# A two-part network on one core: another order of splits, squares and head factors in the hybrid projections, and closing products whose first weight unit goes chunk by chunk

## The reference

```python
h = rmsnorm_2(x, g_mix)
proj = h @ w_in
fq, fk, fv = ...              # 512 columns each: 8 heads of 64
q = rmsnorm_2(q, q_gain)      # per head
k = rmsnorm_2(k, k_gain)
log_f = jax.nn.log_sigmoid(f_logit + b_f)
cum_f = jnp.cumsum(log_f, axis=1)
s = q @ k.T * scale + cum_f[query] - cum_f[key]     # causal
outs.append(softmax(s) @ v)
```

## Time and profile before

| | |
|---|---|
| median of three runs | 2404.61 us (2401.77 to 2405.07) |
| profiled execution, its own time | 2405.37 us |
| its span in the profile | 2403.4 us |
| TensorE busy | 2305.6 us, 96% of the span |
| VectorE, ScalarE, GpSimd busy | 1136.2, 871.9, 363.4 us |

### The profile page before, as it was taken

One profiled execution on the slowest core, in us unless ns is written; L12 is line 12 of the kernel. 1 busy time (PEld: TensorE's weight loads), 2 busy tenths in 40 slices (PEclk: granted clock), 3 DMA queues, 4 the chain that ended last, 5 costly groups with the idle time before them and its releaser, 6 DMA issues.

```text
span 2403.4 us, 26105 instructions
## 1 busy us (share of the span) xinstructions
PE 2305.6 (96%) x10864; PEld 1871.0 (78%) x10864; DVE 1136.2 (47%) x1746; ACT 871.9 (36%) x1290; POOL 363.4 (15%) x319
## 2 busy tenths in 40 slices
PE   7789999999979999999998999999999999999998
PEld 5457888888857678888887867888888788888886
DVE  4894433334224645334345465554233346555552
ACT  4664322223213643222143275552322234333342
POOL 1301210112200002011031302332001111000021
PEclk8799999999989999999999999999999999999999
DMA  3203232323251012232335123225244333332331
GB/s 125 93 13 106 90 103 90 104 88 110 71 175 61 1 50 91 88 105 88 105 79 88 18 23 65 52 46 88 53 88 92 101 89 87 106 105 88 97 97 61
DMA packets 218882, 197.04 MB, mean 82 GB/s; under 512 B 5216, under 2 KB 211500, under 8 KB 218637
## 3 DMA queue, kind: packets, MB, share of 16 engines
q1 hardware_dynamic: 216748, 189.70, 29.8%
q0 software_dynamic: 1504, 5.51, 0.7%
q10 hardware_dynamic: 513, 0.17, 0.0%
HBM read 190.65 MB, written 4.72 MB: 81 GB/s over the span
## 4 chain that ended last, share of the span: by engine, by line
PE 87%; DVE 6%; ACT 4%; DMA 2%; issue 1%; POOL 0%; SPq 0%; POOLq 0%; ACTq 0%; DVEq 0%
PE bank L519 23%; PE bank L521 23%; PE bank L520 23%; PE bank L2091 5%; PE bank L842 2%; PE bank L2277 2%; PE bank L1596 1%; PE bank L693 1%; DVE dsa_latents L1155 1%; DVE small L1153 1%; DVE weight_lo L505 1%; PE bank L1021 1%; PE bank L703 1%; PE bank L1438 1%; ACT hybrid_step L806 1%
## 5 line engine op out<-in xcount | busy, mean ns | idle before, releaser
L519 PE MATMUL bank<-h_hi,weight_hi 128*128 128x512 f32 (+1 forms) x1576 | 622.1, 395 | 12.0 <-DVE weight_lo L505 5.2
L520 PE MATMUL bank<-h_lo,weight_hi 128*128 128x512 f32 (+1 forms) x1576 | 617.3, 392 | 0.0
L521 PE MATMUL bank<-h_hi,weight_lo 128*128 128x512 f32 (+1 forms) x1576 | 617.2, 392 | 0.0
L505 DVE TENSOR_TENSOR weight_lo<-weight_raw,weight_hi 128x2048 fp32r<-128x2048 f32 (+2 forms) x183 | 387.3, 2116 | 410.9 <-ACT weight_hi L496 410.8
L496 ACT ACTIVATE weight_hi<-weight_raw 128x2048 fp32r<-128x2048 f32 (+2 forms) x183 | 321.4, 1756 | 393.6 <-PE bank L521 350.6
L519 PEld LDWEIGHTS bank<-h_hi,weight_hi 128*128 128x128 f32 (+1 forms) x1576 | 298.2, 189 | 76.7 <-issue 11.3
L521 PEld LDWEIGHTS bank<-h_hi,weight_lo 128*128 128x128 f32 (+1 forms) x1576 | 297.9, 189 | 63.8
L520 PEld LDWEIGHTS bank<-h_lo,weight_hi 128*128 128x128 f32 (+1 forms) x1576 | 298.3, 189 | 62.2 <-issue 0.2
L519 PE MATMUL bank<-hidden_hi,weight_hi 128*128 128x512 f32 x512 | 201.8, 394 | 0.0
L521 PE MATMUL bank<-hidden_hi,weight_lo 128*128 128x512 f32 x512 | 200.7, 392 | 0.0
L520 PE MATMUL bank<-hidden_lo,weight_hi 128*128 128x512 f32 x512 | 198.7, 388 | 0.0
(11 more groups left out here) (407 smaller groups left out, 3158.9 us busy)
## 6 DMA issues: line engine op xcount, KB each, us to landing
weight_raw<-in_w_down SPq DMA_DIRECT2D x40, 1024.0 KB, 5.1
weight_raw<-in_w_up SPq DMA_DIRECT2D x32, 1024.0 KB, 5.4
weight_raw<-in_w_up SPq DMA_DIRECT2D x44, 512.0 KB, 4.6
weight_raw<-in_w_in SPq DMA_DIRECT2D x20, 1024.0 KB, 9.0
weight_raw<-in_w_in SPq DMA_DIRECT2D x26, 512.0 KB, 7.1
weight_raw<-in_w_kv_shared SPq DMA_DIRECT2D x6, 1024.0 KB, 4.9
weight_raw<-in_w_branch SPq DMA_DIRECT2D x6, 1024.0 KB, 5.0
weight_raw<-in_a_w_o SPq DMA_DIRECT2D x4, 1024.0 KB, 6.4
```

The costliest lines, as they stand in the source:

```text
L505: dve.e.tensor_tensor(split_flat(v, 1), raw_flat(v), f32(split_flat(v, 0)), ALU.subtract).then_inc(*split.mark(("unit", v)))
L519: pe.e.matmul(o, w[0], x[0], start=start, stop=False)
L520: pe.e.matmul(o, w[0], x[1], start=False, stop=False)
L521: return pe.e.matmul(o, w[1], x[0], start=False, stop=stop)
```

## The change

Two things are changed. In `product_to_stream` the first unit is written chunk by chunk as well: both tiles' banks are opened at once, and chunk k is multiplied into both before chunk k+1. In `mix` and at the start of `fox` the same instructions stand in another order on TensorE, ScalarE and VectorE.

```diff
         def product_to_stream(pe, name, source, freed, ready, st):
-            n = tile = 0
+            n, tile = 1, unit_by_chunk(pe, name, 0, 0, source, freed, ready)
...
+            sums = {2: [0], 3: [1], 4: [2, 3], 6: [4], 7: [5]}
+            spreads = {5: [0], 6: [1, 2], 7: [3]}
             for t in range(2, 8):
                 product_tile(pe, ("fox", t), ...)
-                if t < 6:
-                    tensor_head_sums(pe, t - 2)
-                if t > 4:
-                    tensor_head_spread(pe, t - 5)
-                if t == 7:
-                    tensor_head_sums(pe, 4)
-            tensor_head_spread(pe, 3)
+                for n in sums.get(t, []):
+                    tensor_head_sums(pe, n)
+                for n in spreads.get(t, []):
+                    tensor_head_spread(pe, n)
             for t in range(NT):
                 tensor_fox_values(pe, 0, t)
-                if t < 3:
-                    tensor_head_sums(pe, 5 + t)
+                if t == 0:
+                    tensor_head_sums(pe, 6)
+                    tensor_head_sums(pe, 7)
...
             square(0)
             square(1)
-            scalar_log1p_exp(act, mix, "forget", fl, fe, fu, (mix.dve, ("forget_rows",)))
-            for t in range(2, 8):
-                round_upto(act, unit_at["fox", t // 2] + 1)
-                square(t)
-                if t == 5:
-                    root(0)
-            for t in range(NT):
+            round_upto(act, unit_at["fox", 2])
+            scalar_log1p_exp(act, mix, "forget", fl, fe, fu, (mix.dve, ("forget_rows",)), lambda: square(2))
+            square(3)
+            round_upto(act, unit_at["fox", 3])
+            root(0)
+            square(4)
+            square(5)
+            round_upto(act, unit_at["fox", 4])
+            square(6)
+            square(7)
+            take_values(0, 0)
+            root(1)
+            take_values(0, 1)
+            round_upto(act, unit_at["fox", 5])
+            for t in range(2, NT):
                 take_values(0, t)
-            root(1)
-            round_upto(act, unit_at["fox", 5])
...
+            split_upto(dve, unit_at["fox", 2])
             take(2)
-            vector_log1p_exp(dve, mix, "forget", fe, fu, fd, fox_zero)
-            split_upto(dve, unit_at["fox", 2])
-            take(3)
+            vector_log1p_exp(dve, mix, "forget", fe, fu, fd, fox_zero, lambda: take(3))
+            split_upto(dve, unit_at["fox", 3])
...
+            head_factors(0)
+            take(4)
...
-            take(4)
-            split_upto(dve, unit_at["fox", 3])
             take(5)
-            head_factors(0)
             head_norm(0)
+            split_upto(dve, unit_at["fox", 4])
             take(6)
-            split_upto(dve, unit_at["fox", 4])
...
+            head_factors(1)
             split_upto(dve, unit_at["fox", 5])
-            head_factors(1)
...
         def fox_tensor(pe):
+            for t in range(2):
+                tensor_fox_values(pe, 1, t)
             for h in range(FOX_HEADS + 2):
...
-                if h < 2:
-                    for t in (2 * h, 2 * h + 1):
+                if h == 0:
+                    for t in range(2, NT):
                         tensor_fox_values(pe, 1, t)
```

More of the change, by code:

```diff
@@ L1707, in build_program, with scalar_log1p_exp @@
         ab = const[:, C_FOXAB:C_FOXAB + 4]
-        def scalar_log1p_exp(act, st, name, x, e, u, after):
+        def scalar_log1p_exp(act, st, name, x, e, u, after, between=None):
             by, what = after
@@ L1715, in scalar_log1p_exp, with vector_log1p_exp @@
             act.e.activation(e, e, ACT.Exp, scale=-1.0).then_inc(*st.act.mark((name, "exp")))
+            if between:
+                between()
             act.wait_ge(*st.dve.when(name, "below"))
             act.e.activation(u, u, ACT.Ln).then_inc(*st.act.mark((name, "log")))
-        def vector_log1p_exp(dve, st, name, e, u, d, z):
+        def vector_log1p_exp(dve, st, name, e, u, d, z, between=None):
             dve.wait_ge(*st.act.when(name, "exp"))
```

## The result

The changed kernel runs in 2377.94 us (median of 4 runs, 2377.44 to 2380.47), the kernel before in 2403.49 us (4 runs, 2401.77 to 2405.07): ratio 0.9896, 95% interval 0.9883 to 0.9909. I had said 2382 with a range of 2379 to 2389.

What follows compares the result with a forecast made beforehand. TensorE, busy for 96% of the span, was taken as the bound, so only its idle and slow time could be won. 22.2 + 0.8 + 0.7 = 23.7 us off the profiled 2405.4 gave 2381.7, said as 2382, range 2379 to 2389.

Steps and rivals of the forecast that it cites:

- The three stalls: TensorE idles in `mix` before tile 4 (5.20 us), the first spread (3.5) and the last four spreads (5.89); all go.
- all the signs named for a right forecast: No L693, tile 4 split or second L2677 wait; `mix` clock 1.00; tile 4 to spreads 45 us; values 23 us earlier.
- The links between them: In `mix`, splits, roots and copies would be ready before TensorE wants them: slack 5 us for `fox 2`, 7 for `fox 3`.
- 22.2 for `mix`: Tile 4 to the last spreads ends 22.2 us earlier: 14.6 of idle time, 7.6 of slow stretches behind it.
- 0.8 for the head loop: Value tiles before head 1's logits bring the first product with the values forward by 0.8 us more.
- The 3.05 in this term: Start of the head loop: head 1's logits 1.8 us, the last maximum 0.69, and 0.5 between them.
- 0.7 for o_2: In the closing product o_2, three matmuls of tile 1 fill the second wait, at chunk 1: 0.7 us.
- nothing for the attentions: The two attentions' closing products show no such TensorE wait, so the edit there was costed at nothing.
- No link was late: Rival: a late link, the first spread in `mix` the tightest, costs 5.8 us if all comes back: 2387.5; chance 0.15.
- The meetings of VectorE and GpSimd: Rival: at the head loop's start the two block each other; three meetings cost 2.1 us: 2384; chance 0.08.
- The chunkwise unit's matmuls: Rival: alternating banks delays the first units' 144 matmuls; from 0.16 us each the gain is gone; chance 0.02.

Runs made afterwards that it cites:

- before_again: The kernel before with no edit, run as if it were a changed one: 2402.96 us, ratio 0.9999.
- close_again: The kernel before with only the new chunk-by-chunk closing products (`product_to_stream`), the same edit as close_only: 2402.24 us, ratio 0.9994.
- again: The changed kernel with no edit, run once more against the kernel before: 2377.41 us, ratio 0.9891.
- late_roots: The changed kernel with the first root put back behind tile 5's square and the first head factors behind the take of tile 5: 2384.92 us.
- late_split: The changed kernel with `fox 2` rounded and split behind the forget chain again: 2387.54 us.
- old_head: The changed kernel with the old start of the head loop, the value tiles of the second half behind the first logits again: 2381.81 us, ratio 0.9911.
- close_only: The kernel before with the new `product_to_stream` alone: 2401.06 us, ratio 0.9989.

## Why the prediction was right about the place and wrong about the range

**The three stalls.** Right. Each has been shown by putting it back, and all the signs named for a right forecast came. The links between them held: the split of `fox 2` ends at 1288.31 + 2.29 = 1290.6 and that of `fox 3` at 1300.38 + 2.28 = 1302.7 in the trace of after; the prediction, moved by the 0.9 us by which `mix` starts earlier in this trace, had 1291.5 - 0.9 and 1303.6 - 0.9:

```profile
1288.31 2.29 DVE L505 TENSOR_TENSOR weight_lo<-weight_raw,weight_hi 128x2048 fp32r<-128x2048 f32 x1
...
1300.38 2.28 DVE L505 TENSOR_TENSOR weight_lo<-weight_raw,weight_hi 128x2048 fp32r<-128x2048 f32 x1
```

**22.2 for `mix` and 0.8 for the head loop.** Together 23.0 against 22.7 measured. (The old order took 108.74 to 109.57 us in six traces, the new one 86.70 in four, so 22.5 on average.) By the end of the spreads 67.5 - 45.85 = 21.7 us were won, 0.5 less than the sum: I had put every small group at the 0.80 us of a head sum, but the eight spreads took 6.97 us and not 6.4, the last four of them 1341.75 - 1338.26 = 3.49. Behind the spreads 1.0 came. That isn't what the move of the value tiles is worth, though. With the old head the stretch gains 109.39 - 88.66 = 20.7, so the move gives 2.0: its term was mis-sized by 1.2, since I looked only at ScalarE's wait in the trace of before and not at what an undelayed TensorE runs into next. (The 3.05 in this term is 2.99 by its own parts; nothing hangs on it.)

**0.7 for o_2, nothing for the attentions.** Right in the stretches: 68.19 - 67.49 = 0.70, and no difference in the two others.

**The rivals.** No link was late. The meetings of VectorE and GpSimd cost nothing on the path: head 0's scaling took 2.07 us beside GpSimd, head 1's 1.27 us, and TensorE waited for neither. The chunkwise unit's matmuls run at the pace of the others.

**What failed** is the step from the sum to the time and its range, not a stall or a link. The prediction has "The profiled execution took 2405.4 us, so 2381.7", says of the median that it "is 0.8 lower and inside their spread", and sets the low end at 2379. The 4.1 us between 2382 and 2377.94 are three things.
- 1.1 us is the base. The profiled execution, 2405.37, was the slowest of the four times at hand, and I rounded up from it. The median of three, 2404.61, less 23.7 is 2380.9.
- 1.1 us is the draw of those three. The median of before is 2403.49 with a fourth run and 2403.17 in 33.
- 1.9 us is gain that the sum doesn't hold: the medians lie 25.6 us apart and not 23.7. It isn't in the parts that were changed, which gave 22.7 + 0.7 = 23.4. The stages behind them, below, hold 0.4 to 0.9 us of the rest, and what is left has no place.

Single executions of before go from 2400.21 to 2405.90 (33 runs), mostly by what happens ahead of `mix`: the compression weights, from their first product (L1438) to L1459, took 42.4 to 48.0 us in fourteen traces whose code there is the same. A range around one profiled execution needs this scatter on its lower side too. I gave it 3 us there and 7 on the other, where the rivals were.

The forecast also put everything behind the start of the head loop, but for o_2, at no change. It did change: by +1.1 us of gain at the end, -1.5 over the branch products and +0.8 to +1.3 in the delta-rule stage. Each is about a microsecond and the range held nothing for them, but together they are 0.4 to 0.9 us, so they are the smaller part of the miss.

**What stays open.** The mean of the changed kernel's 8 runs is 2377.9. That of the 19 runs of before that were made beside them is 2403.6, that of the 33 later ones 2403.3: a difference of 25.7 or 25.3, each +- 0.6 (standard error). The stretches, averaged over the traces, account for 22.5 + 0.7 + 1.1 less 0.5 for the branch and delta-rule stretches taken together, 23.8. From 1.5 to 1.9 us remain, which is more than twice the error. Ahead of `mix` the compression weights (to the grouped attention's first logits) took 97.2 us on average in the eight traces with the new order and 98.2 in the six with the old, but with a range of 95.5 to 101.3. It can be scatter there; the runs don't tell.

Open too is what decides whether the clock falls. It isn't the time since the execution's start: `mix` began between 1272.3 and 1277.9 us in the fourteen traces, and neither the 165.1 nor the 41.0 us moved with that, while shifts of 0.7 to 23 us made in `mix` or o_2 did move them. From what the time would have to be counted, or whether it is something else that these kernels share, isn't shown.

## What to carry to other kernels

Where one engine is busy for 96% of the span, list its few waits and ask for each what stands ahead of the releasing step on the releaser's own queue: here weight splits stood behind a reciprocal and a chain for the heads behind a rounding, and reordering by hand gave 1% with no instruction added or removed. Count a stall on TensorE like the three here (4.3 to 6.3 us idle) at its idle time and some 2 us more. When a stall goes, lay out the whole new order from durations and look at what the now earlier engine meets next; start from the median and not from the one profiled execution; and give the forecast a range that also holds the scatter of executions and the clock's changes elsewhere, on both sides.

## What was unexpected of the hardware

A wait of unchanged length can leave TensorE's clock up or bring it down. The same place after the same short waits had a granted clock of 0.50 over 6 us in before_again and of 0.72 in close_again; the stretch around it took 41.0 us in three of fourteen traces and 39.5 to 39.9 in the others. Behind the waits of 2.00 and 0.66 us at the first branch products it stood at 1.00 before the change and at 0.72 over 6 us in again, worth 1.5 us. Of this second place it is shown that a shift of what comes ahead is enough: late_roots, late_split and old_head, with the same lists behind, get the fast stretch back. A move of work in one stage so shifts the time of stages that it doesn't touch, in either direction. And it isn't chance: each kernel's branch and last stretches repeated to 0.15 us where it was traced twice (before, the changed kernel and close_only).
